# One packed word per expert for TensorE's loop, the last hidden turn in the gate bank, and a final norm split over two engines

## The chip, the cores and the metric

The kernel runs on one core of a Trainium2 chip. The metric is device time in microseconds (us) of one execution. Before the change the median of three runs was 1505.0 us (1504.64 to 1505.01).

## What is computed

The reference is two blocks. The first has two layers of mixed attention, retention and mLSTM; the second has one layer with attention and a linear recurrence, and then a mixture of experts. The change touches the mixture and the norm behind it:

```python
logits = (xf @ w_router + b_router)                  # 256 tokens, 32 experts
top_v, top_i = lax.top_k(logits, TOP_K)              # TOP_K = 4
gates = jax.nn.softmax(top_v, axis=-1)
...                                                   # rows sorted by expert
g = xb @ w_gate[e] + b_gate[e]
u = xb @ w_up[e] + b_up[e]
g = jnp.minimum(g, SWIGLU_LIMIT)
u = jnp.clip(u, -SWIGLU_LIMIT, SWIGLU_LIMIT)
glu = g * jax.nn.sigmoid(SWIGLU_ALPHA * g)
y = ((u + 1.0) * glu) @ w_down[e] + b_down[e]         # times the gate, summed per token
...
return rms_norm(x, final_g)                           # 256 x 1024 out
```

All is fp32, D = D_FF = 1024, so each expert has three weights of 4 MB.

## The kernel before, in words

Every engine has its own written-out program, and semaphores order them. The tokens of an expert are taken in blocks of T = 32; how many blocks an expert has (at least 1) is only known at run time. VectorE (DVE) counts them and writes integer tables: `n_blocks` (blocks of each expert), `n_first` (its first block), `n_total`, `n_through` and `hid_at`. The engines read these tables into registers and loop by them.

TensorE (PE) does for each expert e, in `gate_up_then_down` (L1363): `gate_up` for each of e's blocks (L1319: the two halves of the gate and up products at L1215, in between the transposes of the next tokens at L1202 and of the last block's hidden values at L1317, then the gather of tokens at L1196 and the biases at L1233), and then `down` for each block of the expert before (L1340: the old result is added up at L1241, the two halves of the down product at L1225, the gate transposes at L1353). The registers come from three `table` calls (L1358) ahead of these two loops. The experts 1 to 30 stand in a hardware loop of three experts a turn, the last one is written out behind it. Behind the last expert stands the last turn: three more table loads, `turn_hidden` (four transposes into `HTB`, a part of bank 4, where `down` also puts its result), and `down` for the blocks of expert 31. ScalarE (ACT) copies the transposed hidden values out (L757), GpSimd (POOL) copies the ones that are due into `hT_sb` (L545), and `down` waits for that.

Weights come through a ring of nine slots of 2 MB (six loads an expert), issued by SyncE (SP) in `load_turn` (L428). Each load waits until PE has used the slot: for a first half of gate or up (`half_used`), a second half (`ex["g"]`), a first half of down (`down_used`) or a second (`ex["y"]`).

At the end, when the last sum stands in four PSUM banks `OUT`, ACT squares them with a sum (L778), DVE adds eps (L2126), POOL raises to the power -0.5 (L511), DVE multiplies each bank by this and by the norm weight (L2132), and SP stores the two halves of 128 tokens (L488).

Of the kernel before, what the change touches and what calls it, by code (L numbers as in the profile page):

```python
# [31 lines left out]
P = 128  # L32
D = 1024
# [41 lines left out]
MAX_BLOCKS = 64  # L75
TABLE = MAX_BLOCKS + S // T

# [62 lines left out]
def build(nc, ins, out):  # L140
    consts_at = ins["consts_at"]
    ctx = ExitStack()
    with ctx:
        def sb(name, shape, dt=F32):
            return ctx.enter_context(nc.sbuf_tensor(name, shape, dt))
# [18 lines left out]
        def K(name):  # L164
            a, n = consts_at[name]
            return const[:, a:a + n]
# [80 lines left out]
        n_through = sb("n_through", [P, E], I32)  # L247
# [13 lines left out]
        nblk, ncum = piece(E), piece(E)  # L261
# [30 lines left out]
        HTB, XTB = YB[:, 0:QD], YB[:, QD:2 * QD]  # L292

# [32 lines left out]
               "selg", "gt", "gt_out", "bsel", "out")}  # L326
# [52 lines left out]
        def _(sp):  # L379
# [100 lines left out]
            sp.wait_ge(count_ready, 5)  # L480
# [5 lines left out]
            for c in range(TC):  # L486
                sp.wait_ge(x_ready, 2 * DEPTH + 7 + c)
                sp.dma_start(out[0, P * c:P * (c + 1), :], xn[:, c, :]).then_inc(out_done, 16)  # L488
            sp.wait_ge(out_done, 16 * TC)
# [5 lines left out]
        def _(pool):  # L495
# [51 lines left out]
            pool.wait_ge(count_ready, 5)  # L547
# [9 lines left out]
        def _(act):  # L557
# [194 lines left out]
            act.wait_ge(count_ready, 5)  # L752

            def turned_hidden(j):
                at = act.value_load(hid_at[0:1, bass.ds(j, 1)], min_val=0, max_val=(HIDDEN - 1) * QD)
                act.wait_ge(ex["ht"], j + 1)
                A(hT_all[:, bass.ds(at, QD)], HTB, ACT.Copy).then_inc(ex["ht_out"], 1)  # L757
# [14 lines left out]
            turned_hidden(blocks)  # L772
            unread = ring[:, 0, 0:2 * D].rearrange("p (n d) -> p n d", n=4)
            for c in range(TC):
                act.wait_ge(ex["out"], 1)
                for h in range(2):
                    n = 2 * c + h
                    i = A(unread[:, n, :], OUT[n][:, :], ACT.Square, scale=D ** -0.5, accum_out=small[:, 64 + n:65 + n])  # L778
            i.then_inc(act_res, 1)
# [5 lines left out]
        def _(pe):  # L785
# [419 lines left out]
            def gate_up_bank(q):  # L1205

                return (GB if q < 2 else UB)[quarter[q], :]
# [21 lines left out]
            def biases():  # L1229

                for q in range(Q):
                    of = slice(E * (q // 2), E * (q // 2 + 1))
                    mm(gate_up_bank(q), bsel[of, :], bias[of, 512 * (q % 2):512 * (q % 2 + 1)], start=True, stop=False,  # L1233
                       skip_group_check=True)
# [72 lines left out]
            pe.wait_ge(count_ready, 5)  # L1307
# [6 lines left out]
            def turn_hidden():  # L1314

                for c in range(4):
                    i = tp(HTB[:, 2 * T * c:2 * T * (c + 1)], h_sb[:, P * c:P * (c + 1)], ident[0:2 * T, 0:2 * T])  # L1317
                return i
# [38 lines left out]
            def table(t, one, low, high):  # L1357
                return pe.value_load(t[0:1, one], min_val=low, max_val=high)  # L1358
# [5 lines left out]
            def gate_up_then_down(e, one, at, rounds):  # L1364

                before_e = table(n_first, one(e - 1), 0, MAX_BLOCKS - 2)
                downs = table(n_blocks, one(e - 1), 1, S // T)
                count = table(n_blocks, one(e), 1, S // T)
                weights = lambda t: arrived_load(4 + EXPERT_TURNS * at + t, rounds)
                first = before_e + downs  # L1370
                with pe.Fori(0, count) as b:
                    gate_up(before_e, first + b, weights)
                with pe.Fori(0, downs) as b:
                    down(first + count, before_e + b, weights)

# [8 lines left out]
            for at in range(rest):  # L1384
                gate_up_then_down(rounds * RING_EXPERTS + at + 1, static, at, rounds)
# [8 lines left out]
            turn_hidden().then_inc(ex["ht"], 1)  # L1394
# [12 lines left out]
        def _(v):  # L1407
# [643 lines left out]
            v.tensor_copy(n_through[:, :], ncum).then_inc(count_ready, 1)  # L2051
            v.tensor_copy(hid_at[:, :], K("hid_at")).then_inc(count_ready, 1)
# [9 lines left out]
            v.wait_ge(count_ready, 5)  # L2062
# [61 lines left out]
            res.n += 1  # L2124
# [3 lines left out]
            v.wait_ge(roww_in, 48)  # L2128
            for c in range(TC):
                for h in range(2):  # L2130
                    part = slice(512 * h, 512 * (h + 1))
                    i = stt(out=xn[:, c, part], in0=OUT[2 * c + h][:, :], scalar=small[:, 32 + c:33 + c], in1=roww[:, part],  # L2132
                            op0=ALU.mult, op1=ALU.mult)
                    i.then_inc(x_ready, 1) if h else i.then_inc(dve_step, 1)
# [25 lines left out]
```

## Time and profile before

| | |
|---|---|
| median of three runs | 1505.0 us |
| the profiled execution, its own time | 1495.57 us |
| its span, first to last instruction | 1493.7 us |
| PE busy | 1277.2 us (86%) |
| DVE busy | 462.9 us (31%) |
| ACT busy | 207.5 us (14%) |
| mean granted TensorE clock | 0.942 |
| bytes moved by DMA, mean | 466.27 MB, 312 GB/s |
| chain that ended last | PE 66%, DMA 26%, DVE 4%, issue 3% |

The profile comes from one execution. Times on it count from the first instruction. "Issue" in the chain is time in which an engine waited for nothing that the profile shows; PEldq is PE's sequencer, which also runs the table loads and the register operations. A DMA share of 1.00 means that all 16 DMA engines are busy.

### The profile page before, as it was taken

The numbers are of one execution on the slowest core, as the hardware profiler recorded it, in microseconds if no ns is written. First come the engines' busy times: TensorE is split into PE (matmuls) and PEld (weight loads), VectorE is DVE, ScalarE is ACT, GpSimd is POOL, SyncE is SP. The second block draws the span as 40 slices with busy tenths as digits, with TensorE's granted clock in tenths as the row PEclk, the third lists the DMA queues.
The fourth block names the chain that finished last, engine by engine and source line by source line (L and its number), as shares of the span: only waits on it lengthen the run. The fifth ranks groups of instructions, "written<-read, shape, count | busy, mean of one in ns | idle before, by whom it ended". The sixth has DMA issues, their size and how long they took to land.

```text
span 1493.7 us, 27734 instructions
## 1 busy us (share of the span) xinstructions
PE 1277.2 (86%) x10508; PEld 627.3 (42%) x10509; DVE 462.9 (31%) x1076; ACT 207.5 (14%) x497; POOL 44.2 (3%) x77
## 2 busy tenths in 40 slices
PE   7999999998988899999989886676667986986996
PEld 6756576664764523333323332222222332332342
DVE  1525433445484522222322221111112221231322
ACT  1212021111160011111111110010001100100201
POOL 0000000001010100000000000000000000000000
PEclk9999999999999789999999998878888998998999
DMA  9812173131730756999999999999999999999793
GB/s 352 303 57 86 57 281 117 70 124 53 257 113 0 287 236 269 375 406 430 428 428 428 428 428 428 428 428 428 429 429 429 429 429 428 428 428 428 319 429 153
DMA packets 61693, 466.27 MB, mean 312 GB/s; under 512 B 6496, under 2 KB 10332, under 8 KB 36956
## 3 DMA queue, kind: packets, MB, share of 16 engines
q1 hardware_dynamic: 58620, 462.63, 75.1%
q0 software_dynamic: 624, 2.10, 0.4%
q10 hardware_dynamic: 2416, 1.08, 0.3%
q8 instruction: 24, 0.39, 0.1%
q14 instruction: 9, 0.07, 0.0%
HBM read 464.74 MB, written 1.05 MB: 312 GB/s over the span
## 4 chain that ended last, share of the span: by engine, by line
PE 66%; DMA 26%; DVE 4%; issue 3%; ACT 1%; ACTq 0%; POOL 0%; POOLq 0%; DVEq 0%; SPq 0%
DMA ring<-in_w_up_dram 24%; PE bank L1215 19%; PE bank L800 11%; PE bank L807 8%; PE bank L1225 8%; PE bank L973 3%; PE bank L1241 3%; PE bank L1233 3%; PE bank L1196 2%; DMA ring<-in_w_down_dram 2%; PE bank L1162 1%; PE bank L1317 1%; PE bank L1202 1%; PE bank L1353 1%; PE bank L1023 1%
## 5 line engine op out<-in xcount | busy, mean ns | idle before, releaser
L1215 PE MATMUL bank<-ring,mem 128*32 128x512 f32 x2864 | 397.6, 663 | 158.6 <-DMA ring<-in_w_up_dram 107.2
L1215 PEld LDWEIGHTS bank<-ring,mem 128*32 128x32 f32 x2864 | 106.4, 120 | 395.2 <-issue 392.3
L800 PE MATMUL bank<-ring 128*128 128x256 f32 x768 | 168.5, 380 | 0.0
L1225 PE MATMUL bank<-ring,mem 128*32 128x256 f32 x2592 | 156.7, 382 | 2.6 <-DMA ring<-in_w_down_dram 2.1
L800 PEld LDWEIGHTS bank<-ring 128*128 128x128 f32 x768 | 145.3, 190 | 21.1 <-issue 1.7
L807 PE MATMUL bank<-ring 128*128 128x512 f32 (+2 forms) x320 | 124.4, 547 | 4.3 <-DVE ring L1450 4.3
L2082 DVE TENSOR_SCALAR mem<-bank 64x512 f32<-64x512 f32 x48 | 32.8, 682 | 275.4 <-PE bank L1215 275.4
L757 ACT ACTIVATE x_mem<-bank 128x256 f32 x49 | 18.8, 383 | 618.2 <-PE bank L1317 618.2
L1225 PEld LDWEIGHTS bank<-ring,mem 128*32 128x32 f32 x2592 | 76.1, 109 | 63.4 <-issue 18.8
L807 PEld LDWEIGHTS bank<-ring 128*128 128x128 f32 x320 | 62.0, 197 | 61.0 <-issue 52.6
L1241 PE MATMUL bank<-mem,cg 32*128 32x256 f32 x784 | 70.0, 426 | 9.4 <-DVE mem L2102 9.3
L761 ACT ACTIVATE const<-bank 64x512 f32<-64x512 f32 x48 | 28.5, 594 | 230.6 <-PE bank L1215 230.6
L2080 DVE COPY vC<-mem 64x32 f32 x48 | 8.3, 173 | 165.8 <-PE bank L1215 165.8
L1241 PEld LDWEIGHTS bank<-mem,cg 32*128 32x128 f32 x784 | 30.7, 183 | 63.8 <-issue 45.7
L2100 DVE COPY cg<-bank 128x256 f32<-128x256 f32 x48 | 20.4, 425 | 118.9 <-PE bank L1353 118.9
L1196 PE MATMUL bank<-xn,vC 128*32 128x256 f32 x800 | 55.5, 393 | 1.0 <-DVE vC L1963 1.0
L1215 PE MATMUL bank<-x_mem,mem 128*32 128x512 f32 x208 | 54.1, 669 | 0.0
L1233 PE MATMUL bank<-const,vC 32*32 32x512 f32 x392 | 52.8, 605 | 0.5
L2088 DVE SCALAR_TENSOR_TENSOR mem<-const 64x512 f32<-64x512 f32 x48 | 51.4, 1071 | 1.7
L2076 DVE TENSOR_SCALAR vC<-const,mem 128x32 f32<-128x32 f32 x96 | 18.2, 232 | 100.0 <-issue 97.7
L545 POOL COPY mem<-x_mem 128x256 f32 x48 | 19.2, 400 | 952.4 <-PE bank L1225 516.3
L1196 PEld LDWEIGHTS bank<-xn,vC 128*32 128x32 f32 x800 | 26.9, 110 | 40.0 <-issue 29.5
(354 smaller groups left out, 1057.2 us busy)
## 6 DMA issues: line engine op xcount, KB each, us to landing
ring<-in_w_gate_dram SPq DMA_DIRECT2D x64, 2048.0 KB, 30.6
ring<-in_w_up_dram SPq DMA_DIRECT2D x54, 2048.0 KB, 25.9
ring<-in_w_down_dram SPq DMA_DIRECT2D x53, 2048.0 KB, 26.1
ring<-in_w_in_dram SPq DMA_DIRECT2D x19, 2048.0 KB, 11.9
x_mem<-in_w_down_dram SPq DMA_DIRECT2D x11, 2048.0 KB, 24.9
x_mem<-in_w_up_dram SPq DMA_DIRECT2D x10, 2048.0 KB, 32.3
ring<-in_w_out_dram SPq DMA_DIRECT2D x6, 2048.0 KB, 7.9
ring<-in_w_in_dram SPq DMA_DIRECT2D x2, 1056.0 KB, 8.3
```

The source lines that it names most:

```text
L761: A(u_sb, UB[2 * T:4 * T, :], ACT.Copy).then_inc(ex["uc"], 1)
L800: i = mm(b[:, S * j:S * j + S], w[:, k, P * (c + j):P * (c + j + 1)], hT[:, k, :], start=(k == 0), stop=(k == KC - 1))
L807: i = mm(b[:, 0:n], hT[:, k, P * c:P * (c + 1)], w[:, k, 0:n], start=(k == 0), stop=(k == KC - 1))
L973: mm(PJ[2 * c + h][:, :], lhs[:, P * c:P * (c + 1)], w_out[h][:, k, :], start=first, stop=False)
L1196: i = mm(pairs_of(dst[quarter[q], 0:QD]), sel[:, c, :], contracted(xn[:, c, :], q), start=(c == 0), stop=(c == TC - 1), skip_group_check=True)
L1215: i = mm(gate_up_bank(q), xT[:, at:at + T], w[q // 2][:, c, 512 * (q % 2):512 * (q % 2 + 1)], start=False, stop=(h == 1 and c == 3), skip_ ...
L1225: i = mm(YB[quarter[q], 0:QD], hT_sb[:, at:at + T], w[:, c, cols_of[q]], start=(h == 0 and c == 0), stop=(h == 1 and c == 3), skip_group_c ...
L1233: mm(gate_up_bank(q), bsel[of, :], bias[of, 512 * (q % 2):512 * (q % 2 + 1)], start=True, stop=False, skip_group_check=True)
L1241: i = mm(OUT[2 * c + q // 2][:, half], gT[quarter[q], P * c:P * (c + 1)], y_sb[quarter[q], :], start=False, stop=False, skip_group_check=True)
L2082: ts(g_sb, GB[0:2 * T, :], SWIGLU_LIMIT, None, ALU.min).then_inc(ex["gc"], 1)
L2088: stt(out=chunked(h_sb), in0=natural(tanh_g), scalar=1.0, in1=natural(u_sb), op0=ALU.add, op1=ALU.mult).then_inc(ex["h"], 1)
L2100: v.tensor_copy(gT, XGB[:, 0:S]).then_inc(ex["gt_out"], 1)
```

## The change

- PE's loop. DVE writes one more table, `packed`: for expert e the word holds the first block of expert e-1 (6 bits), the blocks of e-1 less one (3 bits) and the blocks of e less one. That is three more DVE instructions of 31 columns each. `gate_up_then_down` loads this one word and takes it apart with register operations. All engines wait for six tables and not for five.
- Last turn. PE takes its register values from the expert before, with no table load. `turn_hidden` writes its transposes into bank 0 (the gate bank), no longer into bank 4, and waits for a new semaphore `ex["bias"]` (the last biases are in that bank) in place of `ex["y_out"]`.
- Final norm. DVE multiplies banks 2 and 3 of `OUT` by the norm weight while ACT squares banks 0 and 1, then they swap. With the factor known, DVE scales tokens 128 to 255 in SBUF in two halves and SP stores each half; ACT scales tokens 0 to 127 and stores them from its own queue.

```diff
@@ PE, per expert
-                before_e = table(n_first, one(e - 1), 0, MAX_BLOCKS - 2)
-                downs = table(n_blocks, one(e - 1), 1, S // T)
-                count = table(n_blocks, one(e), 1, S // T)
+                of_e = table(packed, one(e), 0, PACK_COUNT * (S // T) - 1)
+                before_e = of_e & (PACK_DOWNS - 1)
+                downs = ((of_e >> 6) & (S // T - 1)) + 1
+                count = (of_e >> 9) + 1
@@ PE, last turn
-            last = table(n_first, static(E - 1), 0, MAX_BLOCKS - 2)
-            count = table(n_blocks, static(E - 1), 1, S // T)
-            blocks = table(n_total, slice(0, 1), E, MAX_BLOCKS - 1)
-            pe.wait_ge(ex["y_out"], last + 1)
+            blocks = last + count
+            pe.wait_ge(ex["bias"], blocks + 1)
...
-            turn_hidden().then_inc(ex["ht"], 1)
+            turn_hidden(LAST_HTB).then_inc(ex["ht"], 1)
@@ ACT, end
-            turned_hidden(blocks)
+            turned_hidden(blocks, LAST_HTB)
...
+            act.wait_ge(ex["out"], 1)
+            for n in range(4):
+                if n == 2:
+                    act.wait_ge(ex["weighted"], 2)
+                i = A(unread[:, n, :], OUT[n][:, :], ACT.Square, scale=D ** -0.5, accum_out=small[:, 64 + n:65 + n])
+                i.then_inc(act_res, 1)
+            act.wait_ge(ex["weighted"], 4)
+            act.wait_ge(pow_res, DEPTH * POW_L + 6)
+            for h in range(2):
+                part = slice(512 * h, 512 * (h + 1))
+                i = A(xn[:, 0, part], xn[:, 0, part], ACT.Copy, scale=small[:, 32:33])
+            i.then_inc(x_ready, 1)
+            act.wait_ge(x_ready, 2 * DEPTH + 7)
+            act.dma_start(out[0, 0:P, :], xn[:, 0, :]).then_inc(out_done, 16)
@@ DVE, tables
+            st.go(ts(packed_high[:, 1:E], nblk[:, 1:E], float(PACK_COUNT), -float(PACK_COUNT + PACK_DOWNS), ALU.mult, ALU.add))
+            st.do(stt(out=packed_low[:, 1:E], in0=nblk[:, 0:E - 1], scalar=float(PACK_DOWNS - 1), in1=ncum[:, 0:E - 1],
+                      op0=ALU.mult, op1=ALU.add))
+            tt(packed[:, 1:E], packed_high[:, 1:E], packed_low[:, 1:E], ALU.add).then_inc(count_ready, 1)
@@ DVE, end
+            for n in (2, 3, 0, 1):
+                if n == 0:
+                    res.n += 2
+                    res.wait()
+                c, part = n // 2, slice(512 * (n % 2), 512 * (n % 2 + 1))
+                tt(xn[:, c, part], OUT[n][:, :], roww[:, part], ALU.mult).then_inc(ex["weighted"], 1)
...
+            for h in range(2):
+                part = slice(512 * h, 512 * (h + 1))
+                ts(xn[:, 1, part], xn[:, 1, part], small[:, 33:34], None, ALU.mult).then_inc(xn_ready, 1)
```

PE between two experts, before: the end of the `down` loop, the table loads, and the head of the next `gate_up` loop (ISA is a fused register operation or an assertion).

```order
L1373 REGISTER_ALU
L1373 COMPARE_AND_BRANCH
L1358 REGISTER_ALU
L1358 TENSOR_LOAD n_first
L1358 ISA x2
L1358 TENSOR_LOAD n_blocks
L1358 ISA x3
L1358 TENSOR_LOAD n_blocks
L1358 ISA x2
L1371 UNCONDITIONAL_BRANCH
L1371 ISA
L1361 ISA [waits ex_xt_out]
```

The same place of the changed kernel.

```order
L1386 REGISTER_ALU
L1386 COMPARE_AND_BRANCH
L1370 ISA
L1370 TENSOR_LOAD packed
L1370 ISA x2
L1384 UNCONDITIONAL_BRANCH
L1334 REGISTER_ALU x3
L1334 ISA
L1373 ISA [waits ex_xt_out]
```

Two loads with their fused operations are gone. The three register operations stand behind the branch, so inside the loop: each `gate_up` turn runs them again. `down` likewise has one more ahead of its first wait and two more ahead of its first product.

PE at the last turn, before and then after.

```order
L1373 COMPARE_AND_BRANCH
L1358 TENSOR_LOAD n_first
L1358 ISA x2
L1358 TENSOR_LOAD n_blocks
L1358 ISA x2
L1358 TENSOR_LOAD n_total
L1358 ISA x2
L1389 REGISTER_ALU
L1390 REGISTER_ALU [waits ex_y_out]
L1317 MATMUL bank4<-const,mem1 128x64 [waits ex_h,ex_xt_out,ex_ht_out]
```

```order
L1386 COMPARE_AND_BRANCH
L1401 REGISTER_ALU x3
L1401 ISA
L1329 MATMUL bank0<-const,mem1 128x64 [waits ex_h,ex_ht_out,ex_bias,ex_xt_out]
L1329 MATMUL bank0<-const,mem1 128x64 x3
L1407 UNCONDITIONAL_BRANCH
```

The three loads and the wait for `ex_y_out` are gone from ahead of the transposes, and the bank is another.

DVE at the end of the program, before and then after.

```order
L2102 COPY mem<-bank 128x256 [waits ex_y]
L2121 REGISTER_ALU
L2121 COMPARE_AND_BRANCH
L2126 SCALAR_TENSOR_TENSOR small<-small 128x2 [waits act_res]
L2132 SCALAR_TENSOR_TENSOR xn<-bank,small,roww 128x512 [waits roww_in,pow_res]
L2132 SCALAR_TENSOR_TENSOR xn<-bank,small,roww 128x512 x3
```

```order
L2147 TENSOR_TENSOR xn<-bank,roww 128x512 [waits ex_out,roww_in]
L2147 TENSOR_TENSOR xn<-bank,roww 128x512
L2147 TENSOR_TENSOR xn<-bank,roww 128x512 [waits act_res]
L2147 TENSOR_TENSOR xn<-bank,roww 128x512
L2150 SCALAR_TENSOR_TENSOR small<-small 128x2 [waits act_res]
L2155 TENSOR_SCALAR xn<-xn,small 128x512 [waits ex_weighted,pow_res]
L2155 TENSOR_SCALAR xn<-xn,small 128x512
```

Four of DVE's instructions over whole banks now stand ahead of the eps step, and two shorter ones behind it.

## Rows read from the trace of the kernel before

**Rows 1.** The chain that ended last, in order of time: start us, us, what.
```profile
652.10 1.97 issue
...
1348.43 32.63 DMA ring<-in_w_up_dram
...
1423.24 1.45 issue
...
1458.03 1.37 issue
```

**Rows 2.** Stretches of time: busy time of each engine, PEclk, DMA share, GB/s.
```profile
627.00:630.00 3.00, 2.31 (x38) 1.14 (x34) 0.85 (x2) 0.00 (x0) 0.40 (x1) 1.00 0.84 262
667.00:670.00 3.00, 3.00 (x30) 1.07 (x26) 0.17 (x1) 0.38 (x1) 0.00 (x0) 1.00 0.65 175
670.00:1404.00 734.00, 577.78 (x6082) 217.40 (x6078) 160.40 (x381) 74.93 (x175) 13.61 (x34) 0.91 1.01 428
1404.00:1413.00 9.00, 8.99 (x90) 2.83 (x86) 3.18 (x7) 2.14 (x5) 0.00 (x0) 1.00 0.14 27
```

**Rows 3.** The timeline of SP: start us, us, instruction.
```profile
626.63 0.33 SPq L428 DMA_DIRECT2D ring<-in_w_up_dram  x1
...
667.87 0.34 SPq L428 DMA_DIRECT2D ring<-in_w_up_dram  x1
```

**Rows 4.** PE's sequencer ahead of expert 31, 1456 to 1459.6: ns min/median/max, first and last start.
```profile
L1358 PEldq TENSOR_LOAD <-n_blocks x2: 297/308/318, 1457.7 to 1458.4; - x2
L1358 PEldq TENSOR_LOAD <-n_first x1: 303/303/303, 1457.0 to 1457.0; - x1
...
L1373 PEldq ALU_OP  x1: 32/32/32, 1456.6 to 1456.6; - x1
L1373 PEldq COMPARE_BRANCH  x1: 76/76/76, 1456.7 to 1456.7; - x1
```

**Rows 5.** The timeline of PE at the first change of expert.
```profile
548.04 5.15 PE L1215 MATMUL bank<-ring,mem 128*32 128x512 f32 x32 [2.14 <-issue]
...
553.88 3.64 PE L1215 MATMUL bank<-ring,mem 128*32 128x512 f32 x32
```

**Rows 6.** Stretches of time around two changes of expert.
```profile
652.00:654.00 2.00, 0.10 (x4) 0.00 (x0) 0.42 (x1) 0.00 (x0) 0.00 (x0) 1.00 0.98 418
```

**Rows 7.** PE's sequencer and PE between two `gate_up` turns of one expert.
```profile
L1361 PEldq EVENT_SEMAPHORE  x1: 51/51/51, 1407.6 to 1407.6; - x1
...
1407.91 1.50 PE L1215 MATMUL bank<-ring,mem 128*32 128x512 f32 x12
```

**Rows 8.** The timeline at the last turn.
```profile
1474.80 0.42 DVE L2102 COPY mem<-bank 128x256 f32<-128x256 f32 x1 [1.47 <-PE bank L1225]
...
1475.85 0.43 PE L1317 MATMUL bank<-const,mem 64*128 64x64 f32 x4 [1.11 <-DVE mem L2102]
...
1476.29 0.71 PE L1241 MATMUL bank<-mem,cg 32*128 32x256 f32 x8
...
1477.46 1.93 PE L1225 MATMUL bank<-ring,mem 128*32 128x256 f32 x32 [0.46 <-issue]
```

**Rows 9.** The timeline of the final norm.
```profile
1484.40 0.60 ACT L778 ACTIVATE ring<-bank 128x512 f32<-128x512 f32 x1 [7.61 <-PE bank L1241]
...
1486.85 0.16 DVE L2126 SCALAR_TENSOR_TENSOR small<-small 128x2 f32<-128x2 f32 x1 [4.09 <-ACT ring L778]
...
1487.85 2.73 DVE L2132 SCALAR_TENSOR_TENSOR xn<-bank,small,roww 128x512 f32<-128x512 f32 x4 [0.83 <-POOL small L511]
1489.28 1.66 SPq L488 DMA_DIRECT2D out_dram<-xn  x2
```

**Rows 10.** DMA from 1488 to 1494: GB/s in 40 slices of 0.15 us.
```profile
GB/s 0 0 0 0 0 0 0 0 0 0 0 0 0 0 410 410 410 410 382 410 410 410 246 410 437 410 410 437 437 355 410 191 0 0 0 0 0 0 0 0
```

**Rows 11.** A group by line and shape: busy us, mean ns.
```profile
L1736 DVE TENSOR_SCALAR xn<-xn,small 128x1024 f32<-128x1024 f32 x2 | 1.5, 750 | 0.2 <-POOL small L511 0.2
```

**Rows 12.** The timeline of DVE behind the table writes.
```profile
520.30 0.30 DVE L2055 SCALAR_TENSOR_TENSOR mem<-const,bank 128x144 f32<-128x144 f32 x1 [0.91 <-PE bank L1301]
```

More of the change, by code:

```diff
@@ L75 @@
 MAX_BLOCKS = 64
+PACK_DOWNS, PACK_COUNT = 64, 512
 TABLE = MAX_BLOCKS + S // T
@@ L246, in build @@
         n_blocks, n_first = sb("n_blocks", [P, E], I32), sb("n_first", [P, E], I32)
-        n_through = sb("n_through", [P, E], I32)
+        n_through, packed = sb("n_through", [P, E], I32), sb("packed", [P, E], I32)
         hid_at = sb("hid_at", [P, MAX_BLOCKS], I32)
@@ L260, in build @@
         negL, rsum = piece(TC), piece(TC)
-        nblk, ncum = piece(E), piece(E)
+        nblk, ncum, packed_high, packed_low = (piece(E) for _ in range(4))
         slot_at, slot_gate = piece(TC, TABLE), piece(TC, TABLE)
@@ L325, in build @@
               ("sel", "xs", "xs_out", "xt", "xt_out", "g", "uc", "gc", "eg", "h", "ht", "ht_out", "hs", "y", "y_out", "sum", "added",
-               "selg", "gt", "gt_out", "bsel", "out")}
+               "selg", "gt", "gt_out", "bsel", "bias", "out", "weighted")}
         class Steps:
@@ L484, in _ @@
             reload(static, 4 + rounds * round_turns, rest)
[L486 to L489, printed above, removed]
+            for h in range(2):
+                part = slice(512 * h, 512 * (h + 1))
+                sp.wait_ge(xn_ready, 2 * DEPTH + 3 + h + 1)
+                sp.dma_start(out[0, P:2 * P, part], xn[:, 1, part]).then_inc(out_done, 16)
+            sp.wait_ge(out_done, 16 * 3)
         @block.gpsimd
@@ L1232, in biases @@
                     of = slice(E * (q // 2), E * (q // 2 + 1))
-                    mm(gate_up_bank(q), bsel[of, :], bias[of, 512 * (q % 2):512 * (q % 2 + 1)], start=True, stop=False,
-                       skip_group_check=True)
+                    i = mm(gate_up_bank(q), bsel[of, :], bias[of, 512 * (q % 2):512 * (q % 2 + 1)], start=True, stop=False,
+                           skip_group_check=True)
+                i.then_inc(ex["bias"], 1)
             def add_up(turn):
@@ L1374, in gate_up_then_down @@
                     down(first + count, before_e + b, weights)
+                return first, count
             static = lambda e: slice(e, e + 1)
@@ L1384, in _ @@
             for at in range(rest):
-                gate_up_then_down(rounds * RING_EXPERTS + at + 1, static, at, rounds)
-            last = table(n_first, static(E - 1), 0, MAX_BLOCKS - 2)
-            count = table(n_blocks, static(E - 1), 1, S // T)
-            blocks = table(n_total, slice(0, 1), E, MAX_BLOCKS - 1)
-            pe.wait_ge(ex["y_out"], last + 1)
+                last, count = gate_up_then_down(rounds * RING_EXPERTS + at + 1, static, at, rounds)
+            blocks = last + count
+            pe.wait_ge(ex["bias"], blocks + 1)
             pe.wait_ge(ex["xt_out"], blocks + 1)
@@ L2061, in _ @@
             v.wait_ge(tr_used, n_tr[0])
-            v.wait_ge(count_ready, 5)
+            v.wait_ge(count_ready, 6)
             v.sem_inc(ex["gt_out"], 1)
@@ L2127, in _ @@
                         op1=ALU.add))
[L2128 to L2134, printed above, removed]
+            v.wait_ge(ex["weighted"], 4)
+            for h in range(2):
+                part = slice(512 * h, 512 * (h + 1))
+                ts(xn[:, 1, part], xn[:, 1, part], small[:, 33:34], None, ALU.mult).then_inc(xn_ready, 1)
 _INS = ['x', 'norm_w', 'w_in', 'conv_w', 'conv_b', 'gate_bias', 'ret_norm_w', 'mlstm_norm_w', 'w_out', 'final_norm_w',
```

27 lines of the change are left out of this document (12 added, 15 removed).

## Prediction

> **What bounds the kernel now.** I read the share of the DMA engines over time first, then the chain of waits, then PE's sequencer at the places that the change touches. From 670 to 1404 us the DMA engines are full: share 1.01 at 428 GB/s, while PE is busy for 578 of 734 us [rows 2]. So in that stretch the weights set the time, and whatever PE saves there it waits away again. The chain of waits says the same: its last long piece on a transfer is 32.63 us from 1348.43 on, which ends at 1381.1 [rows 1]. Behind it the transfers fall silent (share 0.14 from 1404 to 1413 [rows 2]), since PE frees slots too slowly, and the chain runs on PE to the end, with pauses named "issue" of 1.45 and 1.37 us where PE goes from one expert to the next [rows 1].
>
> Ahead of 670 it is mixed. The DMA engines pause there whenever PE has not freed a slot: 3.0 x (1 - 0.84) = 0.5 us around 628 and 3.0 x (1 - 0.65) = 1.05 us around 668 [rows 2]. Each pause ends with a load that PE has just released, those of 626.63 and 667.87 [rows 3]. Such a load is what ties the full stretch to PE: if PE gets there earlier, the whole full stretch moves forward.
>
> So three regions count: PE up to the load that starts the unbroken stretch, PE from 1381 on, and the tail.
>
> **Between experts.** Ahead of expert 31 the sequencer starts its loads at 1457.0, 1457.7 and 1458.4 [rows 4], a pitch of 0.68, since each brings fused operations with it; its own run takes 0.30. The array ran dry at 1458.03 and stood for 1.37 [rows 1]. Two loads less are 2 x 0.67 = 1.34 us of sequencer time. Three register operations come in; a register operation starts 0.1 us ahead of the next instruction (1456.6 and 1456.7 [rows 4]), so they cost 0.3. The net is 1.04 us a change of expert, of the 1.37 to 1.45 that the array stands: some 0.35 stays. At the head of a hardware loop turn the pause is longer (1.97 at 652.10 [rows 1]), because an address operation stands between the loads; there I take 1.2.
>
> The rule of the Trainium skill (DMA: Bandwidth & Descriptors, "Latency and other measured facts") gives a tensor load a floor of about 600 ns. By that two loads less would be 1.2 us and the net 0.9 us, an estimate. The trace has 0.30 for the load itself and 0.68 from load to load, so the two differ on the load and nearly agree on the pitch; I take the pitch.
>
> The first change of expert has a price of its own. There the array stood for 2.14 us, and the next 32 matmuls took 5.15 us where the same 32 take 3.64 at 553.88 [rows 5]: 1.5 us went to TensorE's clock falling to its lower level, 1.2 GHz. At 652 the array stood for 1.97 us and the granted clock stayed at 1.00, which is 2.4 GHz [rows 6]. With 1.2 us less the pause at 546 is 0.9, well under the pause that kept the clock, so I take the 1.5 back too: 2.7 us in all. Bounds: 1.2 and 2.7.
>
> **What the register operations cost inside the loops.** Each `gate_up` turn has three more at its head. Between two turns of one expert the sequencer reaches its last wait at 1407.6, takes 0.05, and the array takes its next matmul at 1407.91 [rows 7]: a cover of 0.2 us against 0.3, so 0.1 us a turn comes through. In `down` the three more are covered by the wait for DVE's copy and by the sums that the array still works on; cover gone, it would be 0.3 a turn. Before the load of 626.63 there are three such repeated `gate_up` turns, and from 1381 on three again: 0.3 us each.
>
> **The gain that reaches the full stretch.** The load of 667.87 has four changes of expert ahead of it (546, 590, 629, 652), so PE releases it 2.7 + 1.04 + 1.04 + 1.2 - 0.4 = 5.6 us earlier. But the work that is queued ahead of it began with the load of 626.63, which has only two ahead: 2.7 + 1.04 - 0.3 = 3.4 us earlier. That work now ends at its own time, and the pause of 1.05 us behind it closes, so the unbroken stretch gains the smaller of 5.6 and 3.4 + 1.05 = 4.5 us. Earlier pauses are longer and don't bind. **4.5 us**; without the clock, 3.0.
>
> The three DVE instructions for `packed` stand ahead of the `hid_at` copy. DVE waits for PE for 0.91 us right behind it [rows 12]; three short instructions with one wait are some 0.6. Cost nothing; the cover is that wait, and 0.6 us of PE if it were gone.
>
> **From 1381 on.** Two changes of expert (1423 and 1458): 2 x 1.04 - 0.3 = **1.8 us**. The loads for the last experts were issued some 10 us and more ahead of their use, so they don't become the wait.
>
> **Last turn.** Before, the transposes start at 1475.85, the sums at 1476.29, and the product at 1477.46, after 0.46 us in which it waits for POOL's copy of the hidden values [rows 8]. From the transposes to the product is 1.61 us. Afterwards PE has no loads to do, and the transposes follow the last product directly, at about 1474.75; the hidden values are ready for 1476.36. The sums wait for DVE's copy that starts at 1474.80; elsewhere that means 0.97 us after its start, so 1475.77, and they take 0.65 until the next work can follow: 1476.42. The product is late by the later one: 1477.46 - 1476.42 = **1.0 us**. Next late is DVE's copy, no longer the sequencer. The wait for `ex["bias"]` costs nothing: those biases are over by 1469.3, ahead of a whole `down`.
>
> **Final norm.** Times from ACT's first square (1484.40). Before: DVE's eps step at 2.45, its four passes from 3.45 at 0.68 each, the first store at 4.88 [rows 9]. After: DVE's first two products take 2 x 0.68 = 1.36 (a product with two tensors and no scalar isn't cheaper than L2132 was). ACT's third square, at 1.15 before, waits for them till 1.45, so the squares end 0.3 late and eps stands at 2.75, the power's result at 3.75. Then DVE's pass over 512 columns of SBUF: 0.75 for 1024 [rows 11], so about 0.42. First half store at 4.2, the second at 4.65, ACT's two copies at about 0.6 each and its store at 5.0. The transfers took 0.15 x 18 = 2.7 us without a gap [rows 10], so their first byte decides: it was tied to the store at 4.88, now to the one at 4.2. Before the last store stood at 1489.28 + 1.66 - 0.34 = 1490.6, so 6.2; now 5.0, which no longer limits. I take 0.7 plus a little for the gap between the two issues, **0.8 us**. Bounds: 0.3 (the smaller pieces move slower) and 1.2 (the last store decides).
>
> The Trainium skill speaks against this step (DMA: Bandwidth & Descriptors, "Rules for kernel authors"): transfers over several issuing engines bring no bandwidth, and at least 1 MiB per DMA is best. The trace shows what it would mean here: two stores of 512 KB kept the engines busy throughout, so three have nothing to win but an earlier start; if pieces of 256 KB ran at half speed, it would be 0.6 us less for the step, and it would end near 0.2.
>
> **Sum.** 4.5 + 1.8 + 1.0 + 0.8 = 8.1 us. Against the profiled execution that is 1495.6 - 8.1 = 1487.5. The median of the timed runs stands 9.4 us above it at 1505.0; I carry the difference over: 1496.9. If the timed runs owe it to slower transfers, the pauses ahead of 670 are smaller there and the 4.5 shrinks somewhat, at most by the 1.05.
>
> **Rivals.**
> 1. The full stretch takes no gain: the transfers are bound ahead of 628 in the timed runs too, or something else than PE releases them. Then 1.8 + 1.0 + 0.8 = 3.6: 1501.4. For it: the 9.4 us between profile and median are not explained. Against: both pauses end on PE's release. Chance 0.18.
> 2. The changed words don't do what they say for PE, as the register work stands in the way of most of the 1.04 and only the tail gains: 1.0 + 0.8 = 1.8, and 1503.2. For it: the array keeps 0.35 us of pause anyhow. Against: the pitch of loads is plain in the trace. Chance 0.07.
> 3. Slower: the register operations in the loop bodies come through. In the two regions bound by PE some 10 `gate_up` and 12 `down` turns run, with 3 more operations each, 66 in all. To turn a gain of 8.1 (0.6 already taken off) into a loss of over 3, each would have to cost 11.7 / 66 = 0.18 us uncovered, where the trace shows 0.1 and a cover of 0.2 a turn. At 0.25 each it is 16.5 - 8.7 = 7.8 us slower, 1512.8. Chance 0.05.
> 4. More than forecast: all four changes count (5.6 in place of 4.5) and the tail gives 1.2. Then 9.6: 1495.4. Chance 0.1.
>
> The forecast itself, with or without the clock's 1.5 us (1496.9 to 1498.4), has 0.60.
>
> **How the numbers follow.** The likeliest time is 1496.9. From the slower end the range takes in rival 1 (1501.4) and half a microsecond; from the faster end rival 4 and the same distance again, for repetition of the clock's return elsewhere: 1494.0 to 1502.0. A measurement of this kernel tells about 0.2%, 3 us, from no change. Faster by more: the forecast, rival 4 and rival 1 (3.6, just past the bound, so part of it falls within): 0.85. Within: 0.10. Slower: 0.05.
>
> **What would show it.** Right: in the chain the pauses between experts fall from 1.4 to about 0.4 us, the first from 2.14 to 0.9, with the 32 matmuls behind it at 3.64; the DMA engines have no pause between about 624 and 1400; the last transfer wait ends near 1376.5; from there to ACT's first square it is 2.8 us less than before; from that square to the end 8.4 in place of 9.3. Wrong: pauses of over 0.7 that remain, a pause at 668 that stays as it is, repeated `gate_up` turns with visible idle time of over 0.2 us, or a store whose data runs well over 2.7 us.

## The result, and the profile after

| | before | after |
|---|---|---|
| median | 1501.32 us (16 runs, 1493.0 to 1505.01) | 1493.26 us (16 runs, 1486.59 to 1498.1) |
| ratio after/before | | 0.995, 95% interval 0.9933 to 0.9966 |
| the profiled execution, its own time | 1495.57 us | 1496.68 us |
| its span | 1493.7 us | 1494.9 us |
| mean granted TensorE clock | 0.942 | 0.935 |

The change makes the kernel faster by 0.34 to 0.67%: 7.5 us in the middle of the interval (the two medians lie 8.1 us apart). Four executions in the later timings took 1680 to 6935 us; they are left out of every median and ratio below. The two profiled executions don't show it as they stand: the one of after is 1.2 us longer. That is no contradiction, since executions of one and the same kernel lie up to 12 us apart, and part of that arises in code that the change doesn't touch. The hidden values' first transposes of the expert stage start at 530.02 us in the trace of before and at 535.56 in that of after, ahead of everything that the change does to PE. So I compare stretches that begin and end on the same instruction, and not the spans.

**Between experts.** The chain of waits of the changed kernel, in three places (start us, us, what): the first change of expert with the two turns behind it, the head of a hardware loop turn with the last transfer that the chain waits for, and the last change.

```profile
551.44 1.02 issue
552.46 3.64 PE bank L1226 x32
...
562.41 0.28 issue
...
572.64 0.19 issue
...
1345.27 0.83 issue
...
1349.87 34.31 DMA ring<-in_w_up_dram
1384.18 0.14 issue
1384.32 5.09 PE bank L1226 x32
...
1391.38 0.16 issue
...
1461.10 0.43 issue
```

The pauses between experts fell as they should: the first from 2.14 [rows 5] to 1.02 us, with the 32 matmuls behind it back at 3.64, the last one, ahead of expert 31, from 1.37 [rows 1] to 0.43, that at the head of a hardware loop turn from 1.97 [rows 1] to 0.83. New are the pieces of 0.28, 0.19 and 0.16 us, each between two turns of one expert, where before nothing stood. PE's sequencer at the first of them, two lines of the kernel (ns min/median/max, first and last start):

```profile
L1384 PEldq COMPARE_BRANCH  x1: 221/221/221, 561.5 to 561.5; - x1
...
L1334 PEldq ALU_OP  x3: 36/36/41, 562.0 to 562.2; - x3
L1334 PEldq FUSED_REGOPS  x1: 120/120/120, 562.3 to 562.3; - x1
```

The branch back starts at 561.5, while the array is still at work on the biases, and the next matmul starts at 562.69 all the same: the three operations at 562.0 to 562.2 stand in series with it.

**The full stretch.** Stretches of time of the changed kernel (busy us of each engine, PEclk, DMA share, GB/s):

```profile
630.00:632.00 2.00, 2.00 (x38) 1.12 (x34) 0.42 (x1) 0.00 (x0) 0.00 (x0) 1.00 0.84 213
670.00:673.00 3.00, 3.00 (x36) 0.91 (x28) 0.00 (x0) 0.00 (x0) 0.00 (x0) 1.00 1.01 306
673.00:1406.00 733.00, 581.01 (x6050) 222.06 (x6038) 160.39 (x381) 74.70 (x174) 13.69 (x34) 0.90 1.01 428
1406.00:1418.00 12.00, 11.84 (x114) 4.54 (x115) 3.19 (x7) 2.53 (x6) 0.00 (x0) 1.00 0.15 42
```

In the share, the pause that stood around 668 (0.65 [rows 2]) is gone, though only 306 GB/s are moved there at a share of 1.01; the pause around 630 is as it was. Behind them the transfers run at the same 428 GB/s as before. The load that ends the pause around 630 is in SP's timeline of the changed kernel:

```profile
629.60 0.33 SPq L430 DMA_DIRECT2D ring<-in_w_up_dram  x1
```

Before, it stood at 626.63 [rows 3]. Counted from the first transposes of the expert stage (530.02 before, 535.56 after), it now comes 94.04 us behind them, where it was 96.61.

**Last turn.** The timeline of the changed kernel:

```profile
1476.80 0.46 PE L1329 MATMUL bank<-const,mem 64*128 64x64 f32 x4
1476.93 0.42 DVE L2118 COPY mem<-bank 128x256 f32<-128x256 f32 x1 [1.47 <-PE bank L1236]
...
1477.41 0.71 PE L1253 MATMUL bank<-mem,cg 32*128 32x256 f32 x8 [0.16 <-DVE mem L2118]
1477.94 0.40 POOL L548 COPY mem<-x_mem 128x256 f32 x1 [10.92 <-ACT x_mem L760]
...
1478.44 1.93 PE L1236 MATMUL bank<-ring,mem 128*32 128x256 f32 x32 [0.31 <-issue]
```

The transposes now start ahead of DVE's copy, not 1.05 us behind its start [rows 8]. From one product to the next it is 3.51 us where it was 4.66. Next late is POOL's copy, ready at about 1478.34: PE stands for 0.31 us until 1478.44, which the profile books as issue, and the order of the two times is what says that it waits for POOL.

**Final norm.** The timeline, and below it the DMA engines' rate from 1488 to 1496 us in 40 slices of 0.2 us, the queue of instruction fetches, and the stores (KB each, median us from issue to landing):

```profile
1485.38 0.60 ACT L781 ACTIVATE ring<-bank 128x512 f32<-128x512 f32 x1 [7.61 <-PE bank L1253]
1485.45 2.52 DVE L2147 TENSOR_TENSOR xn<-bank,roww 128x512 f32<-128x512 f32 x4 [1.71 <-PE bank L1253]
...
1488.07 0.16 DVE L2150 SCALAR_TENSOR_TENSOR small<-small 128x2 f32<-128x2 f32 x1
...
1489.58 0.82 SPq L491 DMA_DIRECT2D out_dram<-xn  x2
1490.49 0.39 ACTq L790 DMA_DIRECT2D out_dram<-xn  x1
```

```profile
GB/s 0 0 0 0 0 0 0 0 0 0 0 0 307 389 369 369 399 348 420 492 348 430 389 410 369 144 21 41 20 20 0 0 0 0 0 0 0 0 0 0
...
q14 instruction: 1, 0.01, 0.2%
...
out_dram<-xn SPq DMA_DIRECT2D x2, 256.0 KB, 2.7
out_dram<-xn ACTq DMA_DIRECT2D x1, 512.0 KB, 4.0
```

The engines do what was forecast: the eps step stands 2.69 us behind the first square (forecast 2.75), SP's first store 4.20 (4.2), ACT's store 5.11 (5.0). But from the first square to the end it is 9.51 us, more than the 9.26 of before. The rate shows where it goes: the data flows until 1493.2, and then 20 to 41 GB/s for another 0.8 us, the rate of one DMA engine alone at work, which takes five packets of 4 KB one behind the other at 0.16 us each.

### The profile page after: what moved, and what is told of

It reads as the page before. It is cut to its first block, busy times and chain, and to the rows that moved or that the text cites. A ratio compares the mean times of both kernels' runs of the same rounds, so it can differ in the third digit from the quotient of the medians.

```text
span 1494.9 us, 27883 instructions
## 1 busy us (share of the span) xinstructions
PE 1288.2 (86%) x10508; PEld 638.2 (43%) x10509; DVE 463.8 (31%) x1081; ACT 209.2 (14%) x499; POOL 44.3 (3%) x77
## 3 DMA queue, kind: packets, MB, share of 16 engines
HBM read 464.74 MB, written 1.05 MB: 312 GB/s over the span
## 4 chain that ended last, share of the span: by engine, by line
PE 63%; DMA 30%; DVE 3%; issue 2%; ACT 1%; ACTq 0%; POOL 0%; SPq 0%; POOLq 0%; DVEq 0%
DMA ring<-in_w_up_dram 28%; PE bank L1226 17%; PE bank L811 11%; PE bank L818 8%; PE bank L1236 7%; PE bank L984 3%; PE bank L1244 2%; PE bank L1253 2%; PE bank L1207 2%; DMA ring<-in_w_down_dram 1%; PE bank L1173 1%; PE bank L1034 1%; PE bank L1365 1%; PE bank L1329 1%; PE bank L1213 1%
## 5 line engine op out<-in xcount | busy, mean ns | idle before, releaser
L1226 PE MATMUL bank<-ring,mem 128*32 128x512 f32 x2864 | 403.2, 671 | 150.3 <-DMA ring<-in_w_up_dram 115.9
L1226 PEld LDWEIGHTS bank<-ring,mem 128*32 128x32 f32 x2864 | 113.3, 121 | 386.7 <-issue 383.9
L1236 PEld LDWEIGHTS bank<-ring,mem 128*32 128x32 f32 x2592 | 76.5, 109 | 62.0 <-issue 19.1
## 6 DMA issues: line engine op xcount, KB each, us to landing
ring<-in_w_in_dram SPq DMA_DIRECT2D x19, 2048.0 KB, 11.7
```

What stands on the lines that cost most here:

```text
L1226: i = mm(gate_up_bank(q), xT[:, at:at + T], w[q // 2][:, c, 512 * (q % 2):512 * (q % 2 + 1)], start=False, stop=(h == 1 and c == 3), skip_ ...
L1236: i = mm(YB[quarter[q], 0:QD], hT_sb[:, at:at + T], w[:, c, cols_of[q]], start=(h == 0 and c == 0), stop=(h == 1 and c == 3), skip_group_c ...
```

## The experiments

e1 to e4, e6 and e7 are single executions, so the argument rests on terms of their traces and not on their times. For all of them the same six numbers, read from the start times in each trace: the median distance of two `gate_up` turns of one expert, the distance over the first change of expert, from the first transposes of hidden values in the expert stage to the end of the last transfer that the chain waits for ("to the last wait"), the 32 matmuls right behind that wait ("pass"), from the wait's end to ACT's first square without that pass ("PE's end"), and from that square to the end ("norm"). All us.

| kernel | turn | first change | to the last wait | pass | PE's end | norm |
|---|---|---|---|---|---|---|
| before | 9.88 | 13.60 | 851.0 | 5.00 | 98.34 | 9.26 |
| after | 10.18 | 10.97 | 848.6 | 5.09 | 96.11 | 9.51 |
| e1 words only | 10.18 | 10.98 | 849.0 | 6.59 | 97.35 | 9.25 |
| e2 last turn only | 9.88 | 13.57 | 852.4 | 3.64 | 97.14 | 9.24 |
| e3 norm only | 9.88 | 13.75 | 851.2 | 5.34 | 98.31 | 8.63 |
| e4 SP stores all | 10.16 | 10.97 | 848.6 | 5.06 | 96.20 | 9.51 |
| e5 kept registers | 9.88 | 11.24 | 848.5 | 3.64 | 95.68 | 9.50 |
| e6 fetch moved | 10.18 | 10.97 | 848.0 | 6.49 | 96.09 | 8.62 |
| e7 pause back | 10.20 | 13.67 | 851.1 | 4.95 | 96.15 | 9.50 |
| e8 kept and moved | 9.88 | 11.24 | 847.2 | 5.34 | 95.65 | 8.63 |
| e9 after again | 10.16 | 10.97 | 848.6 | 5.03 | 96.19 | 9.48 |

**e1_words_only.** Before, with the packed word alone.

```diff
-                before_e = table(n_first, one(e - 1), 0, MAX_BLOCKS - 2)
-                downs = table(n_blocks, one(e - 1), 1, S // T)
-                count = table(n_blocks, one(e), 1, S // T)
+                of_e = table(packed, one(e), 0, PACK_COUNT * (S // T) - 1)
+                before_e = of_e & (PACK_DOWNS - 1)
```

> Only the packed word, with last turn and final norm as before. If the three register operations in the loop body are what the repeated gate_up turns lose, the distance from the transposes of one gate_up turn to those of the next, within one expert, is about 10.16 us here as in the changed kernel (before: 9.88), the pause between experts is 0.43 to 0.48 us inside a loop turn and 0.84 at its head, the last turn (from the start of the last but one down product to that of the next, over the transposes) is 4.66 us as before, and from the first final square to the end it is 9.26 us. If the loss belonged to another part (bank or end), the turns would be back at 9.88.

1498.64 us for one execution. The turn of 10.18 us shows that the longer turn belongs to the words alone, and the last turn is 4.68 us, about as before. PE's end is 0.99 us shorter than before, and to the last wait it is 2.1 us less. That the plain time from the transposes to the first square gains only 1.5 us has its reason in the pass right behind the last wait. Its piece of the chain, and PEclk in the stretch from 1383 to 1387 and the one behind:

```profile
1383.41 6.59 PE bank L1216 x32
```

```profile
1383.00:1387.00 4.00, 3.58 (x20) 1.11 (x24) 0.00 (x0) 0.00 (x0) 0.00 (x0) 0.50 0.98 418
1387.00:1391.00 4.00, 3.98 (x40) 1.13 (x35) 0.93 (x2) 0.91 (x3) 0.00 (x0) 0.70 1.02 434
```

The same 32 matmuls behind the same wait take 3.64 us in e2 and 6.59 here, at a granted clock of 0.50, which is 1.2 GHz. So this pass is taken out of the sums from here on.

**e2_turn_only.** Before, with the last turn's edit alone.

```diff
-            last = table(n_first, static(E - 1), 0, MAX_BLOCKS - 2)
-            count = table(n_blocks, static(E - 1), 1, S // T)
-            blocks = table(n_total, slice(0, 1), E, MAX_BLOCKS - 1)
+            blocks = last + count
+            pe.wait_ge(ex["bias"], blocks + 1)
...
-            turn_hidden().then_inc(ex["ht"], 1)
+            turn_hidden(LAST_HTB).then_inc(ex["ht"], 1)
```

> Only the last turn in the gate bank, three table loads per expert kept. Pauses between experts stay at 1.4 us and gate_up turns at 9.88 us; the last turn is 3.5 us as in the changed kernel, if moving the loads out and changing the bank is what gave 1.15 us. Rival: the gain there came from the sequencer being earlier by the packed word; then it is above 4 us.

1494.35 us. The last turn takes 3.51 us (1472.73 to 1476.25), as in the changed kernel. PE's end is 1.20 us shorter than before. With e1's 0.99 that makes 2.19, and the changed kernel has 2.23: the two edits add up, and nothing else of size acts on this stretch. To the last wait it is 1.4 us longer than before although nothing ahead of it was changed; that is how far single executions scatter in this column.

**e3_norm_only.** Before, with the norm's edit alone (DVE's and ACT's parts and the three stores, as in the diff of the change).

```diff
-                    i = stt(out=xn[:, c, part], in0=OUT[2 * c + h][:, :], scalar=small[:, 32 + c:33 + c], in1=roww[:, part],
-                            op0=ALU.mult, op1=ALU.mult)
+                tt(xn[:, c, part], OUT[n][:, :], roww[:, part], ALU.mult).then_inc(ex["weighted"], 1)
```

> Only the final norm split over two engines. From the first final square to the end 9.5 us, 0.25 more than before, with the last store issued some 1.2 us earlier relative to that square than the last store before but landing 4.0 us after its issue. If the long landing in the changed kernel was an accident of that execution, landing is 2.7 us and the stretch is 8.2 to 8.4 us.

1500.42 us. From the first square to the end 8.63 us: 0.63 less than before, where the same code in the changed kernel takes 0.25 more. That is neither the 9.5 of the expectation nor quite its 8.2 to 8.4. So the norm's edit is not the loss by itself.

**e4_store_by_sp.** The changed kernel with all stores on SP's queue.

```diff
-            act.wait_ge(x_ready, 2 * DEPTH + 7)
-            act.dma_start(out[0, 0:P, :], xn[:, 0, :]).then_inc(out_done, 16)
+            sp.wait_ge(x_ready, 2 * DEPTH + 7)
+            sp.dma_start(out[0, 0:P, :], xn[:, 0, :]).then_inc(out_done, 16)
```

> The changed kernel, but SyncE and not ScalarE issues the store of tokens 0 to 127. Theory: the queue of ScalarE makes the store land late (first packet 1.3 us after issue against 0.84, and two engines lag); with SyncE it lands in 2.7 us and the stretch from first square to end is 8.4 us, 1.1 less than in the changed kernel and 0.8 less than before. Rival: the 2 KB rows or the ScalarE copies cost it; then landing stays near 4.0 us and the stretch near 9.5.

1495.91 us, and 9.51 us from the square to the end, as in the changed kernel. My theory that ACT's queue is slow to its first byte and so costs the 0.8 us has fallen. What the traces of after and e4 have and e3 has not is one packet: a fetch of 8 KB of instructions on queue q14. In after it starts at 1491.96 us, in e4 at 1491.19, amid the stores; in e3 at 1499.95, when the kernel is over.

**e5_kept_registers.** The changed kernel, with the unpacked numbers moved once per expert into registers of their own.

```diff
+            regs = {n: pe.alloc_register("kept_" + n) for n in ("before", "downs", "count", "first")}
+            def kept(n, value, low, high):
+                pe.reg_mov(regs[n], value)
+                return pe.snap(regs[n], min_val=low, max_val=high)
...
-                before_e = of_e & (PACK_DOWNS - 1)
+                before_e = kept("before", of_e & (PACK_DOWNS - 1), 0, MAX_BLOCKS - 2)
```

> The changed kernel, but the four numbers unpacked from the word are moved once per expert into kept registers, so that the loop bodies carry no register work. Theory: the three operations at the head of each turn cost it 0.28 us; then a repeated gate_up turn falls from 10.15 back to 9.88 us, the pauses between experts grow from 0.43 to 0.5-0.8 us for four moves more, and from the last transfer wait to the first square, the first pass behind the wait left out, it is 96.11 - 3 x 0.28 + 2 x (0.1 to 0.35) = 95.5 to 96.0 us. Ratio to before about 0.9945, which can't be told from 0.9950. Rival: the longer turn comes from somewhere else (code layout, the loads' order); then the turn stays at 10.15 and only the pauses grow, 96.3 to 96.8 us.

1493.2 us median of 12 runs against 1499.96; ratio 0.9963 (0.9949 to 0.9978). The timeline of PE at the first change of expert and behind it:

```profile
544.57 3.64 PE L1226 MATMUL bank<-ring,mem 128*32 128x512 f32 x32 [1.29 <-issue]
...
553.45 1.06 PE L1244 MATMUL bank<-const,vC 32*32 32x512 f32 x8
554.45 3.64 PE L1226 MATMUL bank<-ring,mem 128*32 128x512 f32 x32
...
563.33 1.06 PE L1244 MATMUL bank<-const,vC 32*32 32x512 f32 x8
564.32 3.64 PE L1226 MATMUL bank<-ring,mem 128*32 128x512 f32 x32
```

The turns are back at 9.88 us with no idle time ahead of the matmuls, the first pause went from 1.02 to 1.29, those ahead of the last two experts from 0.43 to about 0.7, and PE's end from 96.1 to 95.7. The theory holds: the register work in the body was what each repeated turn paid for. To the last wait the 0.5 us that PE is earlier here don't show (848.5 against 848.6 in after). The time can't tell the two kernels apart.

**e6_fetch_moved.** The changed kernel with 24 waits more on DVE, ahead of its first wait of the expert stage.

```diff
             v.wait_ge(count_ready, 6)
+            for _ in range(24):
+                v.wait_ge(count_ready, 1)
             v.sem_inc(ex["gt_out"], 1)
```

> The changed kernel with 24 waits more on DVE, each on a semaphore that has long been there, in DVE's idle time ahead of its first wait of the expert stage. Theory: the final norm of the changed kernel loses some 0.85 us to a fetch of 8 KB of instructions that falls among the stores and holds back one DMA engine; with 24 instructions more ahead of it the fetch falls before the stores, and from the first square to the end it is 8.6 us, as with the norm alone. Rival: the fetch is harmless and the loss lies in the combination with the last turn; then it stays at 9.5 us. Everything ahead of the norm within 0.3 us of the changed kernel.

1488.17 us for one execution; 8.62 us from the first square to the end. The DMA engines from 1479 to 1487 us, in the same view as that of the changed kernel above:

```profile
GB/s 0 0 0 0 0 0 0 0 0 0 0 0 0 0 0 0 0 0 10 369 348 420 359 379 389 451 430 410 369 451 369 410 82 0 0 0 0 0 0 0
...
out_dram<-xn SPq DMA_DIRECT2D x2, 256.0 KB, 2.2
out_dram<-xn ACTq DMA_DIRECT2D x1, 512.0 KB, 3.1
```

The fetch has moved to 1474.97 us, 2.8 us ahead of ACT's first square, where in after it stood 6.6 us behind it, among the stores; the row of q14 is gone from this stretch, and so is the slow tail. The stores land 0.5 and 0.9 us sooner. Not everything ahead of the norm stayed within the expected 0.3 us: to the last wait it is 0.6 us less than in after, and the pass behind it 1.4 more.

**e7_pause_back.** The changed kernel with two table loads more, once.

```diff
+            for _ in range(2):
+                table(n_blocks, static(0), 1, S // T)
```

> The changed kernel with two table loads more of the kind that was taken out, their values unused, once ahead of the loop over experts, so that only the first pause is as long as before. Theory (the clock): the pause goes from 1.02 to about 2.3 us, the granted clock falls, and the pass behind it takes 5.1 in place of 3.64 us; first change 13.6-13.9 in place of 10.97 us. The loss up to the end is then not 2.8 but at most that, since the pause of the transfers around 669 comes back by what the full stretch doesn't need. Rival: the pass of 5.15 us had another cause (the weights' arrival); then it stays at 3.64 us and the first change at 12.3 us.

1493.51 us. The chain at the first change of expert, and the stretch from 548 to 551 us:

```profile
545.89 2.33 issue
548.22 5.04 PE bank L1226 x32
```

```profile
548.00:551.00 3.00, 2.78 (x16) 0.90 (x20) 0.39 (x2) 0.00 (x0) 0.00 (x0) 0.50 1.02 437
```

The long pause brings the slow pass back, at a granted clock of 0.50, with all the rest of the change in place. It was the pause that took the clock down, and two loads less give back their own 1.3 us and 1.4 us of clock. The load that ends the pause around 630 stands 96.64 us behind the first transposes here, 2.6 later than in after, and to the last wait it is 2.5 us more: what is lost at the first change isn't made good later. Both figures are those of before (96.61 and 851.0). So without the gain of the first change, the rest of the words' edit brings the full stretch nothing that shows: what the other pauses give up, the longer turns take.

**e8_kept_and_moved.** Both edits, e5's and e6's.

```diff
+            for _ in range(24):
+                v.wait_ge(count_ready, 1)
...
+                before_e = kept("before", of_e & (PACK_DOWNS - 1), 0, MAX_BLOCKS - 2)
```

> Both: kept registers and the 24 waits on DVE. By the two theories the turns are 9.88 us and the norm 8.6 us, together 1.0 to 1.4 us less than the changed kernel in the profile; ratio to before 0.994 (0.9925 to 0.9955). By the rivals of both it is no faster than the changed kernel, 0.995 to 0.9955.

1491.56 us median of 10 runs against 1499.96; ratio 0.9946 (0.9926 to 0.9966). The trace has both gains (turn 9.88, norm 8.63, PE's end 95.65). The intervals of this kernel and of the changed one overlap, so that it is the better version is shown by the traces' terms, not by the times.

**e9_changed_again.** The changed kernel, unaltered.

> The changed kernel once more, unaltered, as a control. The terms read in the traces sum to some 5.0 us (0.9967), while the first timing gave 7.5 us (0.9950, 0.9933 to 0.9966). If the terms are complete, the ratio comes out between 0.9955 and 0.9975; if the timed executions owe something more to the change, it comes out at 0.995 or below again. In the profile: turn 10.15, first change 10.97, last transfer wait to the first square less the pass behind the wait 96.1, last part 9.5 us.

1495.17 us median of 8 runs against 1500.35; ratio 0.9956 (0.9936 to 0.9976). The ratio falls just inside what was expected if the terms are complete (0.9955 to 0.9975), but its interval holds the other expectation, 0.995, as well, so this run doesn't decide. All six numbers of the trace repeat those of after within 0.1 us.

## Why the prediction was wrong in its level and right in its direction

**The level.** The forecast of 1496.9 us, with a range down to 1494.0, missed the 1493.26 by 0.7 us at its lower end. The step that failed is "I carry the difference over": it took the 9.4 us between the profiled execution and the median of three runs for a lasting property of the timed runs. Those three, 1504.64 to 1505.01, happened to lie close together and near the top. Sixteen runs have their median at 1501.32 and reach from 1493.0 to 1505.01, so the profiled execution was an ordinary one, and the level was 3.7 us too high. As a ratio the forecast was 0.9946, inside the measured interval. That is in part luck: the terms that the traces show come to 5.0 us and not to the 8.1 of the forecast, as the next table tells.

**The sum.** Forecast 8.1 us. The traces, term by term:

| term | forecast | measured |
|---|---|---|
| full stretch | 4.5 | 3.0 |
| from 1381 on, words | 1.8 | 1.0 |
| last turn | 1.0 | 1.2 |
| final norm | 0.8 | -0.25 |
| sum | 8.1 | 5.0 |

- The pauses between experts: right in size. Two loads less for three register operations gave 1.02 us (1.45 to 0.43, ahead of the last but one expert) against a forecast of 1.04. What the Trainium skill states (DMA: Bandwidth & Descriptors, "Latency and other measured facts") would have given 0.9; the pitch of the trace was nearer.
- The first change of expert: right, with its mechanism. Forecast 2.7 us, measured 13.60 - 10.97 = 2.6. e7 shows the clock's part apart from everything else.
- "A cover of 0.2 us against 0.3, so 0.1 us a turn comes through": wrong in size. There is no cover. A repeated turn grew by 0.27 to 0.3 us. I had read the 0.3 us from the sequencer's last wait to the next matmul as slack [rows 7]; it is the way from the one to the other, and whatever stands ahead of the wait is added in full. e5 takes the operations out of the body, and the turn is 9.88 again. Six such turns at 0.2 more than forecast are 1.2 us, over both regions.
- The full stretch: 3.0 in place of 4.5. The mean to the last wait is 851.5 in before, e2 and e3, and 848.6 in after, e1, e4, e6 and e9. Of the 3.0, 2.7 are there already at the load that ends the pause around 630 (96.65 us behind the first transposes against 93.95, means of the same kernels), where the forecast had 3.4; the turns explain 0.5 of the difference. "The pause of 1.05 us behind it closes" is the step that failed: from that load to the last wait the means are 754.9 and 754.6, so the closed pause brought some 0.3. The DMA share is full in that place now, but the rate is 306 GB/s; why the time stays is not shown, and the column scatters by 1.4 within one kind of kernel. By e7 nearly the whole gain of this stretch is that of the first change of expert.
- The three DVE instructions for `packed`: cost nothing, as forecast. DVE's wait for PE behind them is 0.50 us in e5 and e6, down from 0.91 [rows 12], and PE's wait for DVE that follows is 1.00 us in before, after, e5 and e6 alike.
- From 1381 on: 1.0 in place of 1.8, and e1 alone shows the same 0.99. Three repeated turns at 0.28 take 0.8 from the 1.02 and 0.94 of the two pauses, which leaves 1.1.
- Last turn: right, and slightly more. The mechanism was the forecast one, but by the times it is POOL's copy, not DVE's, that PE waits for next, with 0.31 us left.
- Final norm: the engines' part was right to 0.1 us, and by e3 and e6 it is worth 0.63. What was missing is the fetch: with it the step costs 0.25 us. With the new norm, the fetch falls outside the stores in e3, e6 and e8, and there the norm takes 8.62 to 8.63 us; in after, e4, e5, e7 and e9 it falls among them, and the norm takes 9.48 to 9.51. It takes both of the change's additions to DVE's program to bring it there: behind the first square the fetch stands at 10.95 us with the words alone (e1), at 10.33 with the norm alone (e3), both past the kernel's end, and at 6.58 with both. The objection that I had weighed there was that of the Trainium skill (DMA: Bandwidth & Descriptors, "Rules for kernel authors"), more issuing engines and smaller transfers. It isn't what happened: in e6 the same three stores keep the engines at 350 to 450 GB/s throughout. The forecast's price for it was too low besides: by the 2.7 us of the whole output, two pieces of 256 KB at half speed are some 1.3 us more, not 0.6.

**Rivals.** Rival 1 fell: the pauses end on PE, and the full stretch did gain, in the trace and by e7. Rival 2 fell with the pauses of 0.43. Rival 3 had the right mechanism: the operations do come through uncovered, but at 0.09 to 0.10 us each and in `gate_up` turns alone, six times 0.28 us = 1.7 us in all, where a loss of over 3 us would have needed 11.7. The `down` turns in the last region kept their distance (6.0 us between sums in before and after); PE stands for 0.55 us there for DVE's copy. Rival 4 (1495.4) came nearest to the measured time, but not by its terms: the 5.6 of four changes and the 1.2 of the norm did not come, and what brought the time down was the level.

**The signs.** Of the signs of being wrong that the prediction named, two came: a repeated turn with 0.28 us of visible idle time, and a store whose data ran for over 2.7 us. The last wait came at 1384.18 and not near 1376.5, 5.5 us of which this execution had lost ahead of the expert stage.

**What stays open.** The terms sum to 5.0 us. The two timings of the changed kernel gave 7.5 us (5.1 to 10.1) and 0.9956, which is 6.6 us (3.6 to 9.6). The sum lies just below the first interval and inside the second. Whether the executions that nobody profiled owe the change another 1 or 2 us, say because the clock falls more seldom in them, no run here can tell. The sum also leaves out the pass behind the last wait. With the register operations in the loop (after, e1, e4, e6, e7, e9) its mean is 5.5 us, without them (before, e2, e3, e5, e8) 4.6; each group scatters by 1.6 us or more, so whether the change costs something there is open too.

## What to carry to other kernels

Take the level from as many executions as there are, and the gain from stretches between the same two instructions; a median of three can stand 4 us off in a kernel whose executions spread over 12. Register work that is taken out of a load lands where its values are used: look in the order of instructions for whether that is inside a loop's body, and count it in full there unless the engine visibly waits for another one. When a tail of a few us gets slower against its own arithmetic, look for a packet that isn't yours: 24 waits more in DVE's program moved its instruction fetch from 6.6 us behind the first square to 2.8 ahead of it, and that was worth 0.87 us.

## What the runs showed of the hardware

- **An instruction fetch among stores.** When one fetch of 8 KB, which takes 0.31 us itself, falls among the last stores, a DMA engine ends them 0.8 us behind the others, with packets that leave alone, and the kernel ends 0.87 us later (9.51 against 8.63 and 8.62). That it is the engine of the fetch is an inference: the profile doesn't name the engine of a packet. The fetch's place depends on how many instructions DVE has run through: 24 more moved it from 1491.96 in after to 1474.97 in e6, 9.4 us of which are against the first square. The Trainium skill (Runtime: NRT & Kernel Launch, "Instruction fetch mechanics") says that a fetch runs by its own DMA queue and that its cost is mostly hidden. The queue of its own is in the trace (q14); this fetch was not hidden, and what other fetches cost no run here tried. Why 0.31 us of fetch becomes 0.8 of delay wasn't tried either.
- **The clock differs at the same instructions.** The pass behind the last wait for a transfer took from 3.64 to 6.59 us in eleven profiles of kernels that do the same there. The idle time ahead of it doesn't order them: 3.64 us after 2.97 (e5) and 3.27 (e2), about 5.0 after 2.5 to 2.6, 5.34 after 3.51 and 3.75, and 6.49 and 6.59 after 2.76 and 2.66. Well ahead of the change, from 440 to 460 us, PEclk was 1.00 in e6 and 0.91 in after. By the first transposes of the expert stage the traces lie 8.4 us apart (527.13 in e6, 535.56 in after). The two spans, 1486.4 and 1494.9, differ by 8.5 us, so it is ahead of the expert stage that these two executions part. The two stretches, e6 first and after behind it:

```profile
440.00:460.00 20.00, 15.98 (x65) 8.07 (x63) 18.64 (x33) 6.24 (x19) 0.00 (x0) 1.00 0.10 43
```

```profile
440.00:460.00 20.00, 17.42 (x64) 8.60 (x62) 17.10 (x31) 6.04 (x19) 0.00 (x0) 0.91 0.09 39
```
